# A second output unit by block products: three of the four weight units of an MLP quarter instead of two

## The reference, cut to what matters

```python
def sq_relu_mlp(xn, w_in, w_out):        # w_in [1024, 4096], w_out [4096, 1024]
    h = jax.nn.relu(xn @ w_in)
    return (h * h) @ w_out

def second_block(x, ...):
    for i in range(2):
        h = h + attention_i(rms_norm(h, norm_mix_g[i]))
        h = h + sq_relu_mlp(rms_norm(h, norm_mlp_g[i]), mlp_w_in[i], mlp_w_out[i])
    return rms_norm(h, norm_final_g)
```

## Time and profile before

| | us |
|---|---|
| median of 3 timed runs (1867.93 to 1869.55) | 1868.45 |
| the profiled execution | 1870.38 |
| its span, first to last instruction | 1868.6 |
| PE busy | 1854.1 (99%) |
| DVE busy | 1310.7 (70%) |
| ACT busy | 953.1 (51%) |
| POOL busy | 222.5 (12%) |

### The profile page before, as it was taken

The page is one execution under the profiler, slowest core; times in us unless marked ns, Lnnn a source line. Parts: engine busy times, 40 slices in busy tenths (PEclk is TensorE's granted clock), DMA queues, the critical chain, the costliest instruction groups (busy, mean ns, idle before and its releaser), DMA issues.

```text
span 1868.6 us, 28585 instructions
## 1 busy us (share of the span) xinstructions
PE 1854.1 (99%) x10747; PEld 1551.7 (83%) x10747; DVE 1310.7 (70%) x1816; ACT 953.1 (51%) x1222; POOL 222.5 (12%) x254
## 2 busy tenths in 40 slices
PE   9999999999999999999999999999999999999998
PEld 7788878888888887877888999988778788999997
DVE  7767775677357657556575788687788658588877
ACT  6392464555133344444543555555667754456464
POOL 0010022222210023100221111000000021100000
PEclk9999999999999999999999999999999999999999
DMA  7223123897872238722578788734232166855441
GB/s 242 90 86 126 42 68 99 204 217 177 203 179 91 75 104 212 170 83 68 149 199 252 186 264 215 222 107 151 90 108 85 46 180 170 250 150 187 147 175 68
DMA packets 128085, 277.43 MB, mean 148 GB/s; under 512 B 7389, under 2 KB 78941, under 8 KB 121696
## 3 DMA queue, kind: packets, MB, share of 16 engines
q1 hardware_dynamic: 95744, 187.19, 29.2%
q0 software_dynamic: 31936, 88.41, 22.3%
q10 hardware_dynamic: 288, 0.26, 0.0%
HBM read 271.53 MB, written 73.51 MB: 185 GB/s over the span
## 4 chain that ended last, share of the span: by engine, by line
PE 95%; DVE 2%; ACT 1%; DMA 1%; issue 0%; SPq 0%; DVEq 0%; ACTq 0%
PE bank L1189 22%; PE bank L1187 22%; PE bank L1188 22%; PE bank L1627 6%; PE bank L1628 6%; PE bank L1629 6%; PE bank L1315 2%; PE bank L1932 2%; PE bank L1914 1%; PE bank L1321 1%; PE bank L1803 1%; PE bank L1804 1%; PE bank L1805 1%; PE bank L1738 1%; PE bank L1791 1%; DMA consts<-weight_sums 1%
## 5 line engine op out<-in xcount | busy, mean ns | idle before, releaser
L1187 PE MATMUL bank<-n_hi,w_hi 128*128 128x512 f32 x1054 | 424.7, 403 | 1.7 <-DVE w_lo L2028 1.3
L1189 PE MATMUL bank<-n_hi,w_lo 128*128 128x512 f32 x1054 | 417.9, 396 | 0.0
L1188 PE MATMUL bank<-n_lo,w_hi 128*128 128x512 f32 x1054 | 416.8, 395 | 0.0
L2022 ACT ACTIVATE w_hi<-raw 128x2048 fp32r<-128x2048 f32 (+2 forms) x111 | 207.3, 1868 | 341.9 <-PE bank L1189 319.3
L2028 DVE TENSOR_TENSOR w_lo<-raw,w_hi 128x2048 fp32r<-128x2048 f32 (+2 forms) x117 | 261.7, 2236 | 109.0 <-ACT w_hi L2022 107.1
L1188 PE MATMUL bank<-ff_lo,w_hi 128*128 128x512 f32 x688 | 271.6, 395 | 0.0
L1189 PE MATMUL bank<-ff_hi,w_lo 128*128 128x512 f32 x624 | 248.5, 398 | 0.0
L1187 PE MATMUL bank<-ff_hi,w_hi 128*128 128x512 f32 x624 | 245.5, 393 | 0.0
L1187 PEld LDWEIGHTS bank<-n_hi,w_hi 128*128 128x128 f32 x1054 | 198.0, 188 | 54.6 <-issue 5.0
L1188 PEld LDWEIGHTS bank<-n_lo,w_hi 128*128 128x128 f32 x1054 | 198.0, 188 | 48.8 <-issue 2.9
L1189 PEld LDWEIGHTS bank<-n_hi,w_lo 128*128 128x128 f32 x1054 | 197.9, 188 | 46.6
(11 more groups left out here) (467 smaller groups left out, 3319.3 us busy)
## 6 DMA issues: line engine op xcount, KB each, us to landing
weight_sums<-in_mlp_in POOLq DMA_DIRECT2D x72, 512.0 KB, 8.9
consts<-weight_sums SPq DMA_DIRECT2D x68, 512.0 KB, 7.3
raw<-in_w_up SPq DMA_DIRECT2D x22, 1024.0 KB, 5.1
raw<-in_mlp_out SPq DMA_DIRECT2D x22, 1024.0 KB, 5.8
raw<-in_mlp_in SPq DMA_DIRECT2D x24, 768.0 KB, 7.2
weight_sums<-weight_sums POOLq DMA_DIRECT2D x68, 256.0 KB, 6.1
weight_sums<-in_mlp_out POOLq DMA_DIRECT2D x30, 512.0 KB, 8.8
raw<-in_w_units SPq DMA_DIRECT2D x14, 1024.0 KB, 4.8
```

Source lines behind the costliest of these rows:

```text
L1187: nc.tensor.matmul(b[:, :], w_hi[:, j % 2, cols], hi, start=start, stop=False)
L1188: nc.tensor.matmul(b[:, :], w_hi[:, j % 2, cols], lo, start=False, stop=False)
L1189: return nc.tensor.matmul(b[:, :], w_lo[:, j % 2, cols], hi, start=False, stop=final)
L2022: act.activation(w_hi[:, s, cols], raw[:, s, cols], ACT.Copy).then_inc(hi_ready, 1)
```

## The change

The second output unit of the six quarters m = 1, 2, 3, 5, 6, 7 goes by block products too (`FIRST_DOWN`, u = 4; `DOWN` is now u = 5 and `LATE` u = 6). Six more rows of S sums are made, 40 in all, and the four sets of POOL take seven, two, six and five pairs instead of six, two, six and three.

The T sums are made unit by unit (`unit_sums`: one operation of 512 columns and two of 256), each behind the low half of the unit's squares, so those of units 0 to 2 stand within the burst. They are split in two groups, units 0 and 1, and units 2 and 3; the splits of the first group and of FIRST_DOWN's A1 stand on both engines ahead of the last unit's squares. The high part of T1 lies in a free block of `w_hi` and in one of `raw_r`.

Places in `w_hi` and `w_lo`, banks and waits are arranged anew for three block units in a row. For the next quarter's unit 0, A22 is split ahead of S23 on ACT, and on DVE ahead of second_added, last_added and S23. The last plain unit of m = 3 and 7 (`last_down`) is split in two halves and takes its even k tiles first.

The core of the diff:

```diff
-SUM_UNITS = 34
+SUM_UNITS = 40
...
+        T_AT = {"T1": slice(0, 1), "T4": slice(2, 3), "T23": slice(1, 4, 2)}
+        t_near = [w_hi_flat[:, 5 * SEQ:6 * SEQ], raw_r[:, 0, 0:SEQ]]
...
-        DOWN, LATE = UNITS, UNITS + 1
+        FIRST_DOWN, DOWN, LATE = UNITS, UNITS + 1, UNITS + 2
...
+        DOWN_PLACE = {"A11": 6, "A12": 7, "A22": 4, "S2": 2, "S3": 3, "S4": 0, "S1": 1}
+        LATE_PLACE = {**DOWN_PLACE, "S4": 6, "S1": 7}
+        LAST_PLACE = (6, 7, 4, 5)
...
-            return range(UNITS + has_down(m) + has_late(m)) if m % 4 else ()
+            return range(UNITS + 2 + has_late(m)) if m % 4 else ()
...
-        SUM_SETS = ((0, 12), (12, 16), (16, 28), (28, 34))
+        SUM_SETS = ((0, 14), (14, 18), (18, 30), (30, 40))
...
             if u == 0 and has_late(m - 1):
-                piece_used(eng, m - 1, {"A1": ("S4", DOWN), "A22": ("S3", LATE), "S23": ("A22", LATE), "S14": ("S4", LATE)}[op])
+                piece_used(eng, m - 1, {"A1": ("S4", DOWN), "A22": ("S2", LATE), "S23": ("S4", LATE), "S14": ("S1", LATE)}[op])
             elif u == 0:
                 eng.wait_ge(w_used, v - (1 if op[0] == "A" else 0))
-            elif u == DOWN:
-                if op == "S14":
-                    piece_used(eng, m, ("A12", DOWN))
+            elif u == FIRST_DOWN:
+                if op[0] == "S":
+                    eng.wait_ge(w_used, p_dn[m].u0 + 1)
                 else:
-                    eng.wait_ge(w_used, v - (0 if op == "A22" else 1))
-            elif u == LATE:
-                if op == "S23":
-                    piece_used(eng, m, ("S3", DOWN))
-                elif op == "S14":
-                    piece_used(eng, m, ("A11", LATE))
-                else:
-                    eng.wait_ge(w_used, p_dn[m].u0 + 2)
+                    piece_used(eng, m, ({"A1": "S3", "A22": "S4"}[op], u - 1))
+            elif u == LATE and op == "S14":
+                piece_used(eng, m, ("A12", LATE))
+            elif u > FIRST_DOWN:
+                piece_used(eng, m, ({"A1": "A12", "A22": "A22", "S23": "S3", "S14": "S4"}[op], u - 1))
             elif op != "A22":
                 piece_used(eng, m, (LAST_OF_OP[op], u - 1))
 
         def place(name, u):
-            return DOWN_PLACE[name] if u == DOWN else LATE_PLACE[name] if u == LATE else PLACE[name] + (u % 2 if name == "A22" else 0)
+            return PLACE[name] + (u % 2 if name == "A22" else 0) if u < UNITS else (LATE_PLACE if u == LATE else DOWN_PLACE)[name]
 
         def places(v, op, u):
...
-                sp.wait_ge(at("piece_lo"), split_count[m, op, {2: 0, 3: 1, DOWN: 2, LATE: DOWN}[u]])
+                sp.wait_ge(at("piece_lo"), split_count[m, op, {2: 0, 3: 1, FIRST_DOWN: 2, DOWN: FIRST_DOWN, LATE: DOWN}[u]])
...
-                if has_down(m):
+                if quarter:
                     begun_down_tensor(pe, m)
+                    block_tensor(pe, m, FIRST_DOWN)
                     block_tensor(pe, m, DOWN)
                     if has_late(m):
                         block_tensor(pe, m, LATE)
                     else:
-                        plain_down(pe, m, 3)
+                        last_down(pe, m)
                 else:
...
-        def down_sums(dve, m):
-
-            n0 = sum_count[m, T_SUMS[0]] - 1
-            t1, t3, t2, t4 = (t_whole(scratch, name) for name in T_SUMS)
-            done(dve, dve.tensor_tensor(t1, t1, t3, ALU.subtract), at("sums_ready"), n0 + 1)
-            done(dve, dve.tensor_tensor(t3, t2, t3, ALU.subtract), at("sums_ready"), n0 + 2)
-            done(dve, dve.scalar_tensor_tensor(t2, t2, -1.0, t1, ALU.mult, ALU.subtract), at("sums_ready"), n0 + 3)
-            done(dve, dve.scalar_tensor_tensor(t4, t2, -1.0, t4, ALU.mult, ALU.subtract), at("sums_ready"), n0 + 4)
...
+        def unit_sums(dve, m, u):
+
+            v = t_all[:, u]
+            for n, (out, ins) in enumerate(((v[:, 0:2], (v[:, 0::3], None, v[:, 1:2].broadcast_to([P, 2, SEQ // 2]))),
+                                            (v[:, 3], (v[:, 3], -1.0, v[:, 0])), (v[:, 2], (v[:, 3], -1.0, v[:, 2])))):
+                first, turned_by, second = ins
+                if n == 0:
+                    made = dve.tensor_tensor(out, first, second, ALU.subtract)
+                else:
+                    made = dve.scalar_tensor_tensor(out, first, turned_by, second, ALU.mult, ALU.subtract)
+                done(dve, made, at("sums_ready"), sum_count[m, "T", u, n])
+
...
+        def t_split_high(act, m, name, group):
+
+            act.wait_ge(at("sums_ready"), sum_count[m, "T", 2 * group + 1, 2])
+            if (name, group) == ("T1", 0):
+                piece_used(act, m, ("S1", UNITS - 1))
+            elif (name, group) == ("T1", 1):
+                act.wait_ge(lo_ready, p_dn[m].u0 + 1)
+            elif (name, group) == ("T23", 0):
                 piece_split(act, m, "S14", UNITS - 1, "lo")
+            ins = act.activation(t_high(name, group), t_all[:, T_GROUPS[group], T_AT[name], :], ACT.Copy)
             ins.then_inc(at("piece_hi"), 1)
+            piece_split(act, m, (name, group), FIRST_DOWN, "hi")
...
         def down_scalar(act, m):
-            ph = p_dn[m]
-            t_split_high(act, m, "T4")
-            t_split_high(act, m, "T2")
-            piece_high(act, m, "A1", DOWN)
-            piece_high(act, m, "S23", DOWN)
-            t_split_high(act, m, "T3")
-            piece_high(act, m, "A22", DOWN)
+            piece_high(act, m, "A22", FIRST_DOWN)
+            t_split_high(act, m, "T4", 1)
+            t_split_high(act, m, "T23", 1)
+            piece_high(act, m, "S23", FIRST_DOWN)
+            t_split_high(act, m, "T1", 1)
+            first_kept(act, m, FIRST_DOWN)
+            piece_high(act, m, "S14", FIRST_DOWN)
+            for op in ("A1", "A22", "S23", "S14"):
+                piece_high(act, m, op, DOWN)
             first_kept(act, m, DOWN)
-            piece_high(act, m, "S14", DOWN)
-            t_split_high(act, m, "T1")
             if has_late(m):
                 for op in ("A1", "A22", "S23"):
                     piece_high(act, m, op, LATE)
                 first_kept(act, m, LATE)
                 piece_high(act, m, "S14", LATE)
-                for op in ("A1", "S23", "A22", "S14"):
+                for op in ("A1", "A22", "S23", "S14"):
                     piece_high(act, m + 1, op, 0)
             else:
-                split_hi(act, ph.u0 + 3, 1)
+                last_begun_high(act, m)
+                last_high(act, m)
 
         def burst_scalar(act, m):
             for u in range(UNITS):
@@ -2827,10 +2856,13 @@
                 if u + 1 < UNITS:
                     for op in ("A22", "S23", "S14"):
                         piece_high(act, m, op, u + 1)
+            t_split_high(act, m, "T4", 0)
+            t_split_high(act, m, "T23", 0)
+            t_split_high(act, m, "T1", 0)
+            piece_high(act, m, "A1", FIRST_DOWN)
             rectified_unit(act, m, UNITS - 1)
             squared_unit(act, m, UNITS - 1)
             unit_high(act, m, UNITS - 1)
-            split_hi(act, p_dn[m].u0 + 1, 1)
...
         def down_vector(dve, m):
-            ph = p_dn[m]
-            down_sums(dve, m)
-            t_split_low(dve, m, "T4")
-            t_split_low(dve, m, "T2")
+            piece_low(dve, m, "A22", FIRST_DOWN)
+            t_split_low(dve, m, "T4", 1)
+            t_split_low(dve, m, "T23", 1)
+            piece_low(dve, m, "S23", FIRST_DOWN)
+            t_split_low(dve, m, "T1", 1)
+            piece_low(dve, m, "S14", FIRST_DOWN)
+            down_added(dve, m)
             piece_low(dve, m, "A1", DOWN)
+            piece_low(dve, m, "A22", DOWN)
+            first_added(dve, m, FIRST_DOWN)
+            third_added(dve, m, FIRST_DOWN)
             piece_low(dve, m, "S23", DOWN)
-            t_split_low(dve, m, "T3")
-            piece_low(dve, m, "A22", DOWN)
-            down_added(dve, m, 0)
-            down_added(dve, m, 1)
+            second_added(dve, m, FIRST_DOWN)
+            last_added(dve, m, FIRST_DOWN)
             piece_low(dve, m, "S14", DOWN)
-            t_split_low(dve, m, "T1")
             if not has_late(m):
-                split_lo(dve, ph.u0 + 3, 1)
+                last_begun_low(dve, m)
+                last_low(dve, m)
                 return
             piece_low(dve, m, "A1", LATE)
             piece_low(dve, m, "A22", LATE)
@@ -3430,10 +3465,10 @@
             piece_low(dve, m + 1, "A1", 0)
             first_added(dve, m, LATE)
             third_added(dve, m, LATE)
-            piece_low(dve, m + 1, "S23", 0)
             piece_low(dve, m + 1, "A22", 0)
             second_added(dve, m, LATE)
             last_added(dve, m, LATE)
+            piece_low(dve, m + 1, "S23", 0)
             piece_low(dve, m + 1, "S14", 0)
 
         def burst_vector(dve, m):
@@ -3449,14 +3484,19 @@
                 third_taken(dve, m, u)
                 if u:
                     unit_low(dve, m, u - 1)
+                    unit_sums(dve, m, u - 1)
```

(6 more changed lines are left out.)

236 lines of the change are left out of this document (125 added, 111 removed).

## The result

The changed kernel takes 1884.38 us (median of 6 runs, 1881.63 to 1889.68), the kernel before 1869.0 beside it (median of 6): ratio 1.0083, 95% interval 1.0072 to 1.0094. It is slower by 0.8%; forecast was 1884. The profiled execution took 1885.15, its span 1883.1, so 14.5 more than the span before.

A forecast was written before the change was run, and what follows sets the result against it. The matrix engine PE, busy 1854.1 of 1868.6 us, was taken to bound the kernel. 1870.4 - 6.7 + 20.8 - 1.0 + 1.8 + 1.0 = 1886.3 profiled, less 1.93: 1884 us; range 1871 to 1896.

The forecast's parts named there:

- The exchange: PE, six quarters: a plain unit (11.20 us) becomes a unit by blocks (10.08); 6.7 us gained if nothing waits.
- The knots: PE's waits for DVE's later splits in each of six quarters: 3.47 us a quarter, 20.8 in all.
- knot 1: PE's wait for the S2/S3 low split of unit 3, the fourth of a burst: 1.47 us a quarter.
- second knot: PE's wait before the plain unit's last two k tiles, for unit 3's low half behind four splits: 1.82 us.
- Quarter 2's end: The 4.01 us wait and 2.0 of half clock go (-6.1); 9.6 us transfer laps beside GpSimd cost 5.1.
- Transfers at quarters 5 and 6: Two transfer laps at 9 us in place of 4.7, at quarter 5's end and quarter 6's burst: 1.8 us.
- late burst loads: Burst loads late in GpSimd's traffic in quarters 2 and 6: allowance of 0.5 us each, 1.0 in all.
- 1 (sums fit into idle time): DVE's idle time takes the sums of squared rows, so PE has no wait: 1861.8 us; 9 in 100.
- 2: Transfers become the bound, laps of 9 to 11 us beyond two places only: 1896 us; 8 in 100.
- 4: Only one knot holds; about 1.8 us of wait a quarter is left: 1874.5 us; 14 in 100.
- 3 (waits halve the clock): Twelve PE waits of 1.5 to 1.8 us, each followed by 2.0 us lost: up to 1908; 7 in 100.

The follow-up runs named there:

- quiet run: The changed kernel with GpSimd's twenty pairs of weight sums spread otherwise, none built beside quarter 2's end or quarter 6: 1880.90 us, ratio 1.0062 to the kernel before.
- two quiet kernels: Kernel before with GpSimd's weight sums respread, 1864.38 us; changed kernel with them respread, four order moves and DVE's S1/S4 split ahead of two additions, 1857.98 us.
- sums_in_gap: The changed kernel with unit 0's three sums moved ahead of DVE's A22 split for unit 3: 1877.33 us, ratio 1.0046 to the kernel before.
- a22_ahead: The changed kernel with ACT's A22 high half for unit 3 ahead of Relu, Square and high half of unit 1: 1876.23 us, ratio 1.0036.
- low_first: The changed kernel with unit 3's Relu, Square, high and low half ahead of the T4, T2/T3, T1 and A1 splits: 1907.66 us, ratio 1.0210.

## Why the prediction was right

- **The exchange (-6.7).** Right: the quiet run's quarter closes with 1.12, and with the knots undone 6.4 us lie between the two quiet kernels.
- **The knots (+20.8, 3.47 a quarter).** Measured 1.48 + 0.15 + 1.71 = 3.34, 20.0 in all. The loop through Relu carried the 1.64 of a unit's sums on, as the working said; sums_in_gap and a22_ahead show it. In quarter 6 knot 1 was 2.14, with a late transfer in it. The working put the second knot down to the four splits ahead of the low half; its sum held (1.82 forecast, 1.71 measured), but low_first shows that moving them behind the low half is no cure. It did not see either that both knots can be undone without removing any work.
- **Quarter 2's end (-6.1 and +5.1, net -1.0).** The first half was right (no 4 us wait, no half clock), the second too high: PE waited 0.4, 0.7 and 0.7 there, 1.8 in place of 5.1, some 3 us too much. The 9.6 us a lap came from a few transfers, and these scatter by more than the term is worth (3.7 to 12.2 us in the rows above; in the changed kernel a median of 7.5 from 1150 to 1180). The last of the three waits, at 1181.73, ends on DVE's S2/S3 split, which stands behind the additions. With the same order and the quiet spread it is gone, so the order alone does not make it.
- **Transfers at quarters 5 and 6 (+1.8), late burst loads (+1.0).** Measured 0.3 + 0.9 + 0.7 = 1.9 for quarter 6 in one execution. For late burst loads no run has a row: the table has no wait for them.
- **Missing:** the ends of quarters 3 and 7, 1.0 and 1.5 us of waits and 0.5 or more of half clock in the last norm. The prediction gave the last plain unit's order "no matmul" and looked no further; the half split there waits for S1 on PE, and the additions for the norm stand behind it.

Put together by the profiled execution: -6.7 + 20.0 + 3.7 - 6.1 + 2.5 + 0.5 = 13.9 of the 14.5 us between the spans. The sum of the prediction was 15.9. The near-perfect 1884 is thus partly luck: 3.3 too much for the transfers of quarter 2, 1.0 for burst loads and 0.8 for the knots stand against 3.0 that were missing at the ends and about 0.6 not placed. The size of the transfer terms was luck in another way too: they are one execution's, and the runs of the changed kernel lie 8.1 us apart.

The rivals: 1 (sums fit into idle time) falls, since the idle time stayed at 2.12 us. 2 falls in the changed kernel, where late transfers cost 3.7 us and not 12, and 4 falls, since both knots are there in all six quarters. 3 (waits halve the clock) falls for the knots: behind all twelve the clock was 1.00. Here the stretch behind the wait at 1041.26, and that behind the one at 1733.16, 2.14 us long:

```profile
1041.26:1045.00 3.74, 3.74 (x31) 3.74 (x32) 3.57 (x6) 1.47 (x2) 2.49 (x4) 1.00 1.00 406
```

```profile
1733.16:1737.00 3.84, 3.84 (x32) 3.84 (x33) 3.67 (x6) 0.92 (x2) 0.00 (x0) 1.00 1.04 261
```
